# The six matmuls of a chunk in another order: three for one half's PSUM bank, then three for the other's

## The reference

```python
qkv = rms_norm(x, attn_norm) @ w_qkv      # 2048 x 3072: 16 query, 4 key, 4 value heads of 128
# keys and queries are normalised per head; fgate = log_sigmoid(xn @ w_fgate + b_fgate)
mix = fox_attention(q, k, v, cumsum(fgate), ...)   # prompt: causal over 512
                                                   # sample: over 1024 cached keys and 4 new ones
h = x + mix @ w_o                          # 2048 x 2048
y = h + square(relu(rms_norm(h, mlp_norm) @ w_up)) @ w_down   # 2048 x 8192, 8192 x 2048
```

## Time and profile before

| | |
|---|---|
| median of 3 runs | 2344.38 us |
| lowest, highest | 2339.5, 2347.87 us |
| profiled execution: its time | 2339.07 us |
| profiled execution: its span | 2337.5 us |
| mean granted TensorE clock | 0.996 |
| TensorE matmul share of the span | 97% |
| TensorE weight loads | 95% |
| VectorE, ScalarE, GpSimd | 37%, 28%, 8% |
| mean HBM traffic | 98 GB/s |

### The profile page before, as it was taken

One profiled execution on the slowest core, in us unless ns is written; L12 is line 12 of the kernel. 1 busy time (PEld: TensorE's weight loads), 2 busy tenths in 40 slices (PEclk: granted clock), 3 DMA queues, 4 the chain that ended last, 5 costly groups with the idle time before them and its releaser, 6 DMA issues.

```text
span 2337.5 us, 44415 instructions
## 1 busy us (share of the span) xinstructions
PE 2271.7 (97%) x18249; PEld 2215.4 (95%) x18249; DVE 876.2 (37%) x1201; ACT 655.4 (28%) x935; POOL 183.7 (8%) x225
## 2 busy tenths in 40 slices
PE   6999997997999999999999999999999999999998
PEld 5999996776999999999999999999999999999998
DVE  6366665555222533323333323323323323322331
ACT  4232334555222421222122122122212212212222
POOL 5410003443010000000000000000000000000000
PEclk9999999999999999999999999999999999999999
DMA  4333227761332232232332232233233233233233
GB/s 125 98 84 91 82 71 237 249 226 39 102 90 81 81 90 85 87 90 85 87 90 86 85 90 87 84 90 89 81 90 90 81 90 90 81 90 90 82 89 95
DMA packets 393027, 229.39 MB, mean 98 GB/s; under 512 B 16816, under 2 KB 370608, under 8 KB 392960
## 3 DMA queue, kind: packets, MB, share of 16 engines
q1 hardware_dynamic: 390624, 227.40, 33.1%
q0 software_dynamic: 2336, 1.05, 0.3%
HBM read 221.14 MB, written 7.28 MB: 98 GB/s over the span
## 4 chain that ended last, share of the span: by engine, by line
PE 91%; ACT 2%; DVE 2%; SPq 2%; issue 1%; POOL 1%; DMA 1%; DVEq 0%; ACTq 0%; POOLq 0%
PE ps L1275 29%; PE ps L1274 28%; PE ps L1278 28%; PE ps L1398 1%; PE ps L1422 1%; POOL tmp_c L561 1%; PE ps L1469 1%; ACT w_hi L628 1%; PE ps L1451 1%; PE ps L1409 1%; PE ps L1436 0%; ACT sprob L743 0%; SPq L352 0%; DVE s_nmax L1096 0%; PE ps L1458 0%
## 5 line engine op out<-in xcount | busy, mean ns | idle before, releaser
L1274 PE MATMUL ps<-act_lo,w_hi 128*128 128x272 f32 x3360 | 911.5, 289 | 14.3 <-DVE w_lo L873 8.4
L1275 PE MATMUL ps<-act_hi,w_hi 128*128 128x272 f32 x3360 | 908.9, 289 | 0.0
L873 DVE TENSOR_TENSOR w_lo<-w_raw,w_hi 128x1024 fp32r<-128x1024 f32 x338 | 415.2, 1228 | 1175.3 <-ACT w_hi L628 1175.0
L628 ACT CAST w_hi<-w_raw 128x1024 fp32r<-128x1024 f32 x338 | 354.3, 1048 | 1325.4 <-PE ps L1278 1321.8
L1278 PE MATMUL ps<-act_hi,w_lo 128*128 128x272 f32 x3360 | 697.9, 289 | 0.0
L1274 PEld LDWEIGHTS ps<-act_lo,w_hi 128*128 128x128 f32 x3360 | 634.5, 189 | 15.9 <-issue 9.6
L1275 PEld LDWEIGHTS ps<-act_hi,w_hi 128*128 128x128 f32 x3360 | 634.8, 189 | 0.1
L1274 PE MATMUL ps<-u_lo,w_hi 128*128 128x272 f32 x2048 | 553.5, 288 | 1.1
L1275 PE MATMUL ps<-u_hi,w_hi 128*128 128x272 f32 x2048 | 552.6, 289 | 0.0
L1278 PEld LDWEIGHTS ps<-act_hi,w_lo 128*128 128x128 f32 x3360 | 527.2, 189 | 0.0
L1278 PE MATMUL ps<-u_hi,w_lo 128*128 128x272 f32 x2048 | 424.3, 288 | 0.0
(11 more groups left out here) (174 smaller groups left out, 1046.9 us busy)
## 6 DMA issues: line engine op xcount, KB each, us to landing
w_raw<-in_w_up SPq DMA_DIRECT2D x128, 512.0 KB, 4.0
w_raw<-in_w_down SPq DMA_DIRECT2D x128, 512.0 KB, 3.9
w_raw<-in_w_qkv SPq DMA_DIRECT2D x48, 512.0 KB, 3.8
w_raw<-in_w_o SPq DMA_DIRECT2D x32, 512.0 KB, 3.9
v_page<-in_cache_v SPq DMA_DIRECT2D x64, 256.0 KB, 5.2
k_low<-in_cache_k SPq DMA_DIRECT2D x32, 256.0 KB, 4.9
k_high<-in_cache_k SPq DMA_DIRECT2D x32, 256.0 KB, 6.6
x_tok<-in_x_prompt SPq DMA_DIRECT2D x4, 1024.0 KB, 8.3
```

What stands on the lines that cost most here:

```text
L628: nc.scalar.copy(w_hi[:, k % 2], w_raw[:, k % 4]).then_inc(w_hi_made, 1)
L873: nc.vector.tensor_tensor(w_lo[:, k % 2], w_raw[:, k % 4], w_hi[:, k % 2], ALU.subtract).then_inc(w_lo_made, 1)
L1274: pe.matmul(out[:, a, :], wh, l[:, cols], start=start, stop=False)
L1275: pe.matmul(out[:, a, :], wh, h[:, cols], start=False, stop=False)
```

## The change

The loop over the two halves takes in the product with the low weights. A chunk issues all three products of the first half, then all three of the second. The operands, the accumulation flags of each bank's first and last product and the last matmul of the chunk stay as they are.

```diff
--- before.py
+++ after.py
@@ -1273,8 +1273,6 @@
                     cols = slice(a * HALF, (a + 1) * HALF)
                     pe.matmul(out[:, a, :], wh, l[:, cols], start=start, stop=False)
                     pe.matmul(out[:, a, :], wh, h[:, cols], start=False, stop=False)
-                for a in range(2):
-                    cols = slice(a * HALF, (a + 1) * HALF)
                     ins = pe.matmul(out[:, a, :], wl, h[:, cols], start=False, stop=stop)
                 return ins
```

## The result

The changed kernel takes 2349.3 us (median of 14 runs, 2346.83 to 2352.72); the kernel before, in 14 runs, 2343.51 us (2339.5 to 2347.87). The ratio is 1.0024, with a 95% interval of 1.0016 to 1.0032: a loss of 0.24%, 5.8 us between the medians. That is inside the 0.3% that the prediction called no change, and 2349.3 lies in its range; but the interval excludes 1, and the forecast was that nothing would happen.

The account below looks back on a forecast made before the run. TensorE's matmuls in `chunk`, 2704 chunks at 0.7533 us (87% of the span), were taken as the bound. The change adds 0 to the profiled 2339 us; carried to the median of before, that gives 2344 us, range 2334 to 2356.

Parts of the forecast that it names:

- the 0.3% that the prediction called no change: Whole kernel: about 0.3%, 7 us, is what a measurement can tell from no change; same was given 0.73.
- The count of what is added (nothing): Whole kernel: 0 instructions, DMAs, waits and signals added or removed, and no weight load added or saved.
- The sign named for uncovered loads: TensorE would show idle time inside a unit if weight loads came uncovered; +335 us, chance under 0.01.
- The sign that a chunk's pace moves by over 2.6 ns: In `chunk` on TensorE: such a move, 7 us over 2704 chunks, would make the forecast wrong.
- the exchange of junctions: Per chunk, two steps between matmuls changing the bank alone go, two keeping bank and changing weights come; priced at 0.
- the bounds that the text gave it: For the exchanged steps between matmuls over 2704 chunks: from -19.7 to +22.2 us, with 0 taken between them.
- The argument for 0: In `chunk`, a steady 125.6 ns a matmul with a ripple: what one step gains the next gives back.
- the third rival: Chunks at 0.7533 us go to the output projection's 0.7570: +8.7 us, 2353 us; chance 0.06.
- The first rival: Bank switches in `chunk` cost 1.9 ns each; two fewer a chunk give 10 us less, 2334 us; chance 0.11.
- cycling through banks: A page's warning that cycling PSUM banks with brief idling drops the clock; little to get back expected.
- The second rival: Between line 1275 and the low-weights line, keeping bank and changing weights costs 128.1 ns: +13.5 us, 2358 us; chance 0.10.
- The rule of one load for many matmuls: Weights stay put across matmuls: two loads a chunk before, four after; +335 us by it, but the trace has six either way.

Follow-up runs that it names:

- the fifth to the eighth experiment: Changed kernel with banks alternating, 2351.52 us; alternating order's operands with banks 000111, 2332.73; changed kernel with high weights only, 2350.95; changed kernel with only column halves alternating, 2331.77.
- The second profile of the kernel before: The kernel before, unedited, profiled once more: 2344.03 us.
- the timed kernel with six switches a chunk: Order aH bH aH bH aL bL (a, b banks; H, L weights), against the kernel before: 2333.97 us against 2343.15, ratio 0.9958.
- the eighth experiment: Changed kernel with only the column halves read altered, 010101 instead of 000111; banks, weights and activation tiles stay: 2331.77 us.
- the seventh: Changed kernel with its low-weights product computed with the high weights, so all six loads of a chunk read the same tile: 2350.95 us.
- the repeated chunk address: Changed kernel with each unit's eight chunks all reading the activations of the unit's first chunk: 2334.32 us.

## Why the prediction was wrong

What bounds the kernel was right: TensorE's dense matmuls, whose pace is all that the edit touches; the result is their pace times their number. The count of what is added (nothing) held: instructions, loads, DMAs, waits and idle time are the same. The sign named for uncovered loads, idle time inside a unit, did not appear. The sign that a chunk's pace moves by over 2.6 ns did: 3.0 ns in the mean, 3.3 near 980 us.

The step that failed is the exchange of junctions, priced at 0; it cost 3.0 ns a chunk, 8.1 us, which lies within the bounds that the text gave it. (Their upper end is a little off: 505.2 + 2 x 128.1 is 761.4, not 761.6, so +8.0 ns a chunk and +21.6 us.) Junctions were sorted by bank and weights, and the two kinds of the sort were weighed with care; both are without effect, as the fifth to the eighth experiment show. What the edit also changes, and what the text named only in passing ("input columns"), is the order in which the column halves are read: a a b b a b before, a a a b b b after. With the first order the pace is 753.3 or 756.7 ns a chunk, with the second it was 756.7 in every stretch that was profiled.

The argument for 0, that what one junction gains the next gives back while the chunk keeps its sum, was right about the steps and wrong in its conclusion: the chunk's sum has a few possible values, and the order of reading decides which they are. The two stretches of the earlier trace rows showed two of them for the same code. That was the sign. It was read as stage against stage, and the third rival, the ripple locking elsewhere, had its price from it: 8.7 us, 2353 us, at a chance of 0.06. This rival came about in every stage; the profiled executions differ by 9.6 us, of which the pace makes 8.1. Its reason against ("no reason ties one to the order") is what was false. The medians moved by less, 5.8 us. The second profile of the kernel before, with four of nine stretches at the slow pace, suggests why: the kernel before is itself at that pace part of the time. Its 8 us of spread could have hinted at it but doesn't prove it, since the changed kernel spreads by 5.9 us with no second pace seen.

The first rival, a price of bank switches, is refuted: banks alternating with the changed kernel's operands took 2351.52 us, and two switches a chunk with the alternating operands 2332.73. The Trainium skill's page TensorE: Matmul & The Clock Gate, on cycling through banks (section A second HAM failure mode: psum-queue depth-cycling), wasn't to be seen here: the mean granted clock is 0.995 in the timed kernel with six switches a chunk, and that kernel is the fastest of those that compute the whole. The second rival, the unseen junction of kept bank and changed weights, is refuted by the eighth experiment, which has two of them a chunk and takes 2331.77 us. Its sign, a step of 127 ns or more, was there near 640 us (127.3), but was given back by the step before it. The rule of one load for many matmuls on the same page of the Trainium skill (section Part 2: What happens when you issue a matmul) stays untested, for every kernel here has one load for each matmul. But four changes of weights a chunk are not what the changed kernel pays for: the seventh has none within a chunk, and 0.7571 us.

What stays open is why there are such values at all. The paces of two chunks, 12 matmuls, are 1506.7 and 1513.3 ns in the kernel before; they differ by 6.7 ns, 16 cycles at the granted 2.4 GHz. Why TensorE's stream settles at such steps no run here shows. In the profiles a new one is picked only where the stream has waited; what in the wait picks it, and whether another engine's accesses have a part, was not varied.

## What to carry to other kernels

Where matmuls follow each other without a gap, sum their starts over many and compare stretches of the same code: two paces for the same instructions mean that an edit which adds nothing can move the pace too. Look for the change of pace at the last wait of the stream, and compare whole stretches between such waits. When an order of matmuls is changed, list every address that changes its place in the sequence, beside banks and weights, and begin with the operand that streams through (here the activations). With two column halves to one weight tile, alternating the halves cost nothing here and was worth 0.4%.

## What the runs showed that was not expected

A 272-column matmul with its load took 124.5 to 126.7 ns depending on the order and the start addresses of its columns: chunks of 0.7469 to 0.7605 us, a spread of 1.8% with the same numbers of instructions, the granted clock at 1.00 and no wait in the stretches read. Shifting one half's start by 64 bytes (1024 instead of 1088 after the other) moved it from 0.7565 to 0.7534 us. And one execution of a kernel holds several paces: 0.7534 and 0.7570 us in neighbouring stretches of the kernel before, 0.7469 and 0.7605 us with the repeated chunk address. Once settled, a pace held for some 190 us until the next wait, and a wait of 0.4 us was enough to change it.
